# The odd layer's output projection in two halves of rows, one of them laid as half-token pieces into the ticks of differential attention

## The chip, the cores and the metric

The kernel runs on one NeuronCore of a Trainium2 chip. The metric is device time in microseconds (us). The engines are TensorE (PE, matmuls; PEld are its weight loads), VectorE (DVE), ScalarE (ACT), GpSimd (POOL) and SyncE (SP, which issues the weight DMAs). DVE, ACT, POOL and PE each run their own list of instructions in order, and semaphores tie the lists together.

## What is computed

One inference step of a two-layer decoder trunk for 512 prompt tokens and 64 sample tokens (T = 576 columns), model width 1024. Each layer is FFN, token mixing, FFN, and a gated per-layer input, every one with a residual add. The odd layer mixes by differential attention (4 heads of 128) beside stick-breaking attention (8 heads of 64), and ends in one output projection over both:

```python
cq, ck, cv, sq, sk, sv = jnp.split(hn @ W['od_w_in'][j], SPLIT_ODD, axis=-1)
oc = diff attention of (cq, ck, cv), each head normed and scaled     # 512 features
os_ = stick-breaking attention of (sq, sk, sv)                       # 512 features
mix = jnp.concatenate([oc, os_], axis=-1).astype(hn.dtype) @ W['od_w_out'][j]
h = h + mix
```

The projection is thus a sum of two products: 512 rows of the weight by the differential half and 512 rows by the stick-breaking half.

## The kernel before

**Layout.** Features lie on the 128 partitions and tokens along the free dimension. A product of two fp32 matrices is made of three fp32r matmuls (`mm3`, L574 to L576): high times high, high times the rest, the rest times high. Each operand X is split into a rounded part (`xr`, `wr`) and the rest (`xl`, `wl`). One matmul covers `HALF` = 288 columns, so an output tile of 128 features over K input blocks is K x 2 halves x 3 matmuls.

**Weights.** They come in blocks of at most 2048 columns in two slots. SP loads a block into `raw[s]` (L446), ACT copies it rounded into `wr[s]` (`round_block`, L1124), POOL subtracts to get `wl[s]` (`low_parts`, L559). ACT rounds a block only when PE has done with what the slot held. For the odd output projection (phase `("out", 1)`) a block is two output tiles of 8 input blocks each, and there are four blocks.

**Order in the odd layer.** 22 ticks of stick-breaking attention (`sb_tick`), with the input projections of differential attention cut in pieces between them, 24 matmuls a piece; then 25 ticks of differential attention (N = 20 maps, four heads of four prompt blocks and one group of sample rows, `MAPS`, and 5 ticks to drain); then the head norms; then the output projection. In tick t

- PE makes the scores of map t (L1039, L1044 for sample rows, L1050 else), turns the probabilities of map t-3 into PSUM bank 4 or 5, in turn (`turn_rows`, L876, L878), and multiplies those of map t-4 with the values (L1069 for sample rows, L1078 else);
- DVE adds the bias and takes the maxima of map t (L2038, L2042), then makes the probabilities of map t-1 (`probs`: L2057 and L2059 for sample rows, L2063 to L2068 else);
- ACT takes the exponentials of map t (L1503) and copies the turned rows of map t-3 to `rowsT` (`copy_rowsT`, L343). At the end of each head it copies its output to `oq` (L1520), and the outputs of stick-breaking attention are split into `xr` and `xl` in ticks 3 to 7 (L1490 on ACT, L2136 on DVE).

The buffers `rows` and `rowsT` lie in the weights' slot 1 (`wr[1]`, `wl[1]`), so slot 1 holds no weights during these ticks. After them PE sums squares for the head norms (L1094), ACT takes logarithm and exponential (L1527, L1530), DVE scales each head (L2192), and ACT and DVE split it into `xr` and `xl` (L1490, L2136), each head in turn. PE begins the projection with the four stick-breaking blocks of tile 0, which are ready, and waits for the four heads one by one:

```python
gemm(("out", 1), xin(5), lambda tile, k: ("mix_ready", KD + k + 1) if tile == 0 else None)
```

For each of the 8 output tiles DVE adds the tile to `h` (L1971), ACT makes the rounded next input and the square (L1155, L1145), DVE makes the rest (L1572) and sums the square (L1581):

```python
e.tensor_tensor(two(h[:, j, :]), unit(j % 2), two(h[:, j, :]), ALU.add).then_inc(S("tile_evacuated"), 1)
rest(m, j)
add_square(m, j, False)
```

PE may start tile j when tile j-2 has been added.

Of the kernel before, what the change touches and what calls it, by code (L numbers as in the profile page):

```python
# [85 lines left out]
def schedule():  # L86
    Phase.blocks = Phase.tiles = 0
    ph = {}
    order = []

    def add(name, *a):
        ph[name] = Phase(*a)
        order.append(name)

    def ffn(n):
        at = 0
        for c, k in enumerate(CHUNKS):
            add(("up", n, c), "up", n * sum(CHUNKS) + at, k, (KD, KD))
            at += k
            add(("down", n, c), f"down{c}", n * KD, KD, (k,))  # L100

    for l in range(2):
        ffn(2 * l)
        if l == 0:
            add("glu", "mixin", 0, 4, (KD, KD))
            add("kv", "mixin", 4, 4, (KD, KD))
            add("qo", "mixin", 8, 4, (KD, KD))
        else:
            add("qk1", "mixin", 18, 4, (KD, KD))
            add("v1", "mixin", 22, 2, (KD, KD))  # L110
            add("qk0", "mixin", 12, 4, (KD, KD))
            add("v0", "mixin", 16, 2, (KD, KD))
        add(("out", l), "mixout", l * 4, 4, (KD, KD))
        ffn(2 * l + 1)
        add(("ple", l), "ple", l * KD, KD, (KD, KP))
    return ph, order

def build(nc, A):
# [60 lines left out]
    def x_slot(m):  # L180
# [41 lines left out]
    z = [ZONE]  # L222
    oq = [sb(f"oq{i}", [P, TM, T], at=z) for i in range(2)]
    ok = [sb(f"ok{i}", [P, TM, T], at=z) for i in range(2)]
    ov = [sb(f"ov{i}", [P, ST, DA], at=z) for i in range(2)]
    qs = sb("qs", [P, HEADS, NB, 2, TB], at=z)
    nones = sb("nones", [P, P], at=z)
    identr = sb("identr", [P, P], F32R, at=z)
# [10 lines left out]
             for k in range(2)]  # L239
# [14 lines left out]
    qbd = sb("qbd", [P, 2, 5 * 64], at=z2)  # L254
    assert z2[0] <= XR_AT + 2 * KD * T * 4

    rows, rowsT = ([nc.alloc_sbuf_tensor_at(f"{n}{k}", [P, SEQ], F32, offset=W_AT[1] + (q * 4 + k) * SEQ * 4)
                    for k in range(4)] for q, n in enumerate(("rows", "rowsT")))
    assert 4 * SEQ <= BLK
    rows2 = [tg, sg, tu, hd]  # L260
    srow = sq
    assert max(ENDS) <= END, ("zone", [END - x for x in ENDS])
# [57 lines left out]
    def sample_softmaxes(u):  # L320

        return sum(m[3] == SAMPLES for m in MAPS[:min(u, N)])

    def score_bank(u, c):

        return 2 * (u % 2) + c
# [5 lines left out]
    def copy_rowsT(e, u):  # L332

        e.wait_ge(S("rows_turned"), u + 1)
        if u >= 4:
            e.wait_ge(S("values_done"), u - 3)
        dst, b = rowsT[u % 4], 4 + u % 2
        w = width(u)
        if MAPS[u][3] == SAMPLES:
            w = NPG * 64  # L340
            e.activation(dst[0:SMP, w:w + 64], ps[0:SMP, b, w:w + 64], ACT.Copy).then_inc(S("rowsT_part"), 1)
            e.wait_ge(S("rowsT_part"), SAMPLE_AT.index(u) + 1)
        e.activation(dst[:, 0:w], ps[:, b, 0:w], ACT.Copy).then_inc(S("probsT_copied"), 1)  # L343
# [97 lines left out]
    def _(e):  # L441
# [8 lines left out]
        def load_pair(p, i):  # L450
            for s in range(2):
                load_block(p, i, s)
# [48 lines left out]
        def load_odd(p, p0, pv):  # L501

            load_pair(p0, 0)
            e.wait_ge(S("pages_loaded"), 16)
            e.wait_ge(S("tile_done"), done_at("qk1", 0))
            load_sb_keys(0)
            load_sb_keys(1)
            load_pair(p0, 1)
            load_sb_keys(2)
            load_sb_keys(3)  # L510
            load_block(pv, 0, 0)
            load_sb_keys(4)
            load_sb_keys(5)
            load_sb_keys(6)
            load_block(pv, 0, 1)
            load_sb_keys(7)
            load_sb_values(0)
            load_block(p, 0, 0)
            load_sb_values(1)
            load_sb_values(2)  # L520
            load_block(p, 0, 1)
            for b in range(3, NB):
                load_sb_values(b)
            load_strips()
            for pair in range(PAIRS):
                if pair < 2:
                    e.wait_ge(S("sb_summed"), nth(NU))
                    e.wait_ge(S("sb_values_done"), units_before(NU, PROMPT))
                    e.wait_ge(S("sb_values_used"), NB)
                else:  # L530
                    e.wait_ge(S("values_done"), SAMPLE_AT[pair - 2] + 1)
                load_cache(pair)
            with e.Fori(1, p.nb // 2) as i:
                load_pair(p, i)

        for name in order:
            p = ph[name]
            if name in ("qk0", "v0"):
                continue
            if name == ("out", 1):  # L540
                load_odd(p, ph["qk0"], ph["v0"])
                continue
            with e.Fori(0, p.nb // 2) as i:
                load_pair(p, i)
# [25 lines left out]
    def _(e):  # L570
# [296 lines left out]
        def turn_rows(u, src, w, other=None):  # L867

            e.wait_ge(S("probs_done"), u + 1)
            if u >= 2:  # L870
                e.wait_ge(S("probsT_copied"), u - 1)
            nblk = (w + P - 1) // P
            for b in range(nblk):
                wb = min(P, w - b * P)
                if other is None:
                    mm = e.transpose(ps[0:wb, 4 + u % 2, b * P:(b + 1) * P], src[:, b * P:b * P + wb], C("ident"))  # L876
                else:
                    mm = e.matmul(ps[0:wb, 4 + u % 2, b * 64:(b + 1) * 64], src[:, b * P:b * P + wb], other,  # L878
                                  start=True, stop=True)
            mm.then_inc(S("rows_turned"), 1)  # L880

# [135 lines left out]
            sb_tick(k)  # L1017
        e.wait_ge(S("turned_copied"), 32)

        for tick in range(N + 5):  # L1020
            if tick < N:
                u = tick
# [11 lines left out]
                if i == SAMPLES:  # L1034
                    bank = score_bank(u, 0)
                    both = [(b, slice(64 * b, 64 * b + 64)) for b in range(2)]
                    for hh_ in range(HEADS):
                        for b, r in both:
                            e.matmul(ps[r, bank, 0:PAST], qbd[:, b, hh_ * 64:(hh_ + 1) * 64],  # L1039
                                     kc[hh % 2][:, b, hh_, :, :].rearrange("p g s -> p (g s)"),  # L1040
                                     start=hh_ == 0, stop=hh_ == HEADS - 1)
                    for hh_ in range(HEADS):
                        for b, r in both:
                            mm = e.matmul(ps[r, bank, PAST:KEYS], qbd[:, b, hh_ * 64:(hh_ + 1) * 64],  # L1044
                                          ok[0][:, hh_, SEQ:T], start=hh_ == 0, stop=hh_ == HEADS - 1)
                    mm.then_inc(S("scores"), 1)
                else:
                    for c_ in range(2):
                        r = slice(64 * c_, 64 * c_ + 64)
                        e.matmul(ps[:, score_bank(u, c_), 0:w], oq[0][r, hh, i * P:(i + 1) * P],  # L1050
                                 ok[0][r, hh, 0:w], start=True, stop=True).then_inc(S("scores"), 1)
            if 3 <= tick < N + 3:
                u = tick - 3
                turn_rows(u, rows[u % 4], width(u), C("fold") if MAPS[u][3] == SAMPLES else None)
# [41 lines left out]
            mm.then_inc(S("oc_ss"), 1)  # L1096
        e.wait_ge(S("oc_logged"), 2)

        gemm(("out", 1), xin(5), lambda tile, k: ("mix_ready", KD + k + 1) if tile == 0 else None)
        ffn(3, 6)  # L1100
        ple(1)
        norm_sum(8)
# [3 lines left out]
    def _(e):  # L1106
# [260 lines left out]

        def out_phase(name, m):

            for n in blocks(name):  # L1370
                for j in (2 * n, 2 * n + 1):
                    head(m, j, (S("tile_evacuated"), evac_at(name, j)))
                    square(m, j, None)

# [105 lines left out]
        def mixed_high(j):  # L1480
# [8 lines left out]
                src = oq[0][:, j - HEADS, :]  # L1489
            e.activation(xr[:, j, :], src, ACT.Copy).then_inc(S("mixr_ready"), 1)  # L1490

        for k in range(SB_TICKS):
            sb_act(k)
        for t in range(4):
# [2 lines left out]
        for tick in range(N + 5):  # L1497
# [23 lines left out]
                                 ).then_inc(S("attn_copied"), 1)  # L1521
            if 3 <= tick < 3 + HEADS:
                mixed_high(tick - 3)
        for hh in range(HEADS):
            buf = rows2[hh]
            e.wait_ge(S("oc_ss"), hh + 1)
# [5 lines left out]
                mixed_high(HEADS + hh - 1)  # L1532
        mixed_high(KD - 1)

        out_phase(("out", 1), 6)
        e.wait_ge(S("kv_stored"), 32)
        ffn(3, 6)
        ple(1)
# [12 lines left out]
    def _(e):  # L1551
# [587 lines left out]
        def copy_sb_samples():  # L2139
# [8 lines left out]
            settle()  # L2148
            ins.then_inc(S("sb_samples_copied"), 1)

        hg = tiny[:, 32:32 + HEADS]
        step(e.tensor_scalar(hg, W("head_g", 0, HEADS), 1.0 - LAM_INIT, None, ALU.mult))
        sb_queries()
# [3 lines left out]
            e.wait_ge(S(f"v_stored{t}"), 32)  # L2157
        e.wait_ge(S("turned"), 16)
        odd_tables()
        sample_queries(0)  # L2160
        for tick in range(N + 5):
            if tick < N:
# [19 lines left out]
                copy_sb_samples()  # L2182
            if 4 <= tick < 4 + HEADS:
                mixed_low(tick - 4)
        e.wait_ge(S("attn_copied"), HEADS)
        e.wait_ge(S("sample_copied"), PAIRS)
        e.wait_ge(S("rows_turned"), N)
# [6 lines left out]
            if hh:  # L2194
                mixed_low(HEADS + hh - 1)
        mixed_low(KD - 1)
        out_and_norm(("out", 1), 6)
        ffn(3, 6)
        ple(1)
        e.wait_ge(S("root_ready"), 9)  # L2200
# [164 lines left out]
```

## Time and profile before

| | us |
|---|---|
| median of 3 runs | 2659.73 (2658.12 to 2660.66) |
| the profiled execution | 2663.18 |
| its span in the trace | 2661.4 |
| ticks of differential attention in the trace | 2013.76 to 2097.57 |
| output projection, first matmul to last tile done | 2104.51 to 2156.5 |

Times in the trace count from the start of the span. In the trace's groups a line such as "2113.45 3.43 DVE L1572" is one instruction or a run of like ones: start, duration, engine, source line, operation, output from inputs.
### The profile page before, as it was taken

The numbers are of one execution on the slowest core, as the hardware profiler recorded it, in microseconds if no ns is written. First come the engines' busy times: TensorE is split into PE (matmuls) and PEld (weight loads), VectorE is DVE, ScalarE is ACT, GpSimd is POOL, SyncE is SP. The second block draws the span as 40 slices with busy tenths as digits, with TensorE's granted clock in tenths as the row PEclk, the third lists the DMA queues.
The fourth block names the chain that finished last, engine by engine and source line by source line (L and its number), as shares of the span: only waits on it lengthen the run. The fifth ranks groups of instructions, "written<-read, shape, count | busy, mean of one in ns | idle before, by whom it ended". The sixth has DMA issues, their size and how long they took to land.

```text
span 2661.4 us, 44264 instructions
## 1 busy us (share of the span) xinstructions
PE 2553.7 (96%) x18378; PEld 2436.5 (92%) x18378; DVE 816.2 (31%) x1383; ACT 762.6 (29%) x895; POOL 810.3 (30%) x210
## 2 busy tenths in 40 slices
PE   7999999998789999999999999999997999999997
PEld 7999999986489999999999999998774799999997
DVE  3220222686642211223322022212224522102233
ACT  4221224222523221224422122322232432212233
POOL 3333333321023333333333333431110133343332
PEclk9999999988889999999999999999998999999998
DMA  4223213411112222222221221232124122222222
GB/s 152 79 80 104 79 60 115 88 49 47 50 66 80 79 71 95 87 68 79 99 79 67 93 93 61 97 122 88 64 80 133 66 91 81 75 89 84 70 79 75
DMA packets 67829, 220.85 MB, mean 83 GB/s; under 512 B 13894, under 2 KB 33222, under 8 KB 52106
## 3 DMA queue, kind: packets, MB, share of 16 engines
q1 hardware_dynamic: 51104, 200.61, 21.9%
q10 hardware_dynamic: 16618, 18.70, 2.5%
q8 instruction: 82, 1.34, 0.2%
q14 instruction: 25, 0.20, 0.0%
HBM read 207.95 MB, written 11.33 MB: 82 GB/s over the span
## 4 chain that ended last, share of the span: by engine, by line
issue 79%; POOL 15%; PE 4%; DMA 0%; POOLq 0%; ACT 0%; DVE 0%; SPq 0%; DVEq 0%; ACTq 0%
POOL wl L559 15%; PE ps L574 1%; PE ps L575 1%; PE ps L576 1%; POOLq L565 0%; DMA raw<-in_up 0%; DMA kring<-in_kc 0%; ACT wr L1124 0%; DVE h L2206 0%; PE ps L888 0%; PE ps L634 0%; POOLq L555 0%; PE ps L931 0%; PE ps L891 0%; PE ps L946 0%
## 5 line engine op out<-in xcount | busy, mean ns | idle before, releaser
L559 POOL TENSOR_TENSOR wl<-raw,wr 128x2048 fp32r<-128x2048 f32 (+3 forms) x206 | 810.1, 3934 | 1824.0 <-ACT wr L1124 1824.0
L574 PE MATMUL ps<-xr,wr 128*128 128x288 f32 x4096 | 1219.7, 298 | 30.8 <-POOL wl L559 24.8
L575 PE MATMUL ps<-xl,wr 128*128 128x288 f32 x4096 | 1215.2, 297 | 0.0
L576 PE MATMUL ps<-xr,wl 128*128 128x288 f32 x4096 | 1212.8, 296 | 0.0
L574 PEld LDWEIGHTS ps<-xr,wr 128*128 128x128 f32 x4096 | 776.0, 189 | 36.8 <-issue 27.9
L575 PEld LDWEIGHTS ps<-xl,wr 128*128 128x128 f32 x4096 | 776.4, 190 | 0.8
L576 PEld LDWEIGHTS ps<-xr,wl 128*128 128x128 f32 x4096 | 777.0, 190 | 0.0
L1124 ACT ACTIVATE wr<-raw 128x2048 fp32r<-128x2048 f32 (+1 forms) x200 | 351.8, 1759 | 326.0 <-PE ps L576 283.7
L575 PE MATMUL ps<-hl,wr 128*128 128x288 f32 x1408 | 415.3, 295 | 0.0
L576 PE MATMUL ps<-hr,wl 128*128 128x288 f32 x1408 | 415.0, 295 | 0.0
L574 PE MATMUL ps<-hr,wr 128*128 128x288 f32 x1408 | 413.2, 293 | 0.0
L574 PEld LDWEIGHTS ps<-hr,wr 128*128 128x128 f32 x1408 | 264.7, 188 | 0.9 <-issue 0.9
L575 PEld LDWEIGHTS ps<-hl,wr 128*128 128x128 f32 x1408 | 264.7, 188 | 0.0
L576 PEld LDWEIGHTS ps<-hr,wl 128*128 128x128 f32 x1408 | 264.5, 188 | 0.0
L1179 ACT ACTIVATE hr<-hd 128x576 f32 (+1 forms) x88 | 60.3, 686 | 570.7 <-DVE hd L1616 570.7
L1600 DVE TENSOR_TENSOR tu<-ps,R 128x576 f32<-128x576 f32 x96 | 72.7, 757 | 491.2 <-PE ps L576 491.2
L1600 DVE TENSOR_TENSOR tg<-ps,R 128x576 f32<-128x576 f32 x111 | 84.0, 757 | 337.8 <-PE ps L576 309.8
L1629 DVE SCALAR_TENSOR_TENSOR h<-ps,h 128x576 f32 x64 | 48.5, 758 | 411.7 <-PE ps L576 411.7
L1176 ACT ACTIVATE sg<-tg 128x576 f32<-128x576 f32 x88 | 60.5, 687 | 253.7 <-DVE tg L1600 253.6
L1155 ACT ACTIVATE xr<-h,prm 128x576 fp32r<-128x576 f32 (+1 forms) x64 | 49.7, 776 | 248.6 <-DVE h L1629 167.2
L1620 DVE TENSOR_TENSOR hl<-hd,hr 128x576 f32 x88 | 66.8, 759 | 90.6 <-ACT hr L1179 90.6
L1738 DVE SCALAR_TENSOR_TENSOR ps<-up,prm,ps 128x512 f32<-128x512 f32 x116 | 87.6, 755 | 3.4 <-DVE us L1774 0.9
(338 smaller groups left out, 1431.8 us busy)
## 6 DMA issues: line engine op xcount, KB each, us to landing
raw<-in_up SPq DMA_DIRECT2D x88, 1024.0 KB, 4.7
raw<-in_down SPq DMA_DIRECT2D x32, 768.0 KB, 4.3
raw<-in_mixin SPq DMA_DIRECT2D x24, 1024.0 KB, 4.7
raw<-in_down SPq DMA_DIRECT2D x32, 640.0 KB, 3.8
raw<-in_ple SPq DMA_DIRECT2D x16, 640.0 KB, 3.8
raw<-in_mixout SPq DMA_DIRECT2D x8, 1024.0 KB, 5.0
kring<-in_kc SPq DMA_DIRECT2D x16, 256.0 KB, 4.1
vring<-in_vc SPq DMA_DIRECT2D x16, 256.0 KB, 3.0
```

What stands on the lines that cost most here:

```text
L559: ins = e.tensor_tensor(wl[s][:, c], raw[s][:, c], wr[s][:, c].bitcast(F32), ALU.subtract)
L574: e.matmul(out, wrt, xrt, start=first, stop=False)
L575: e.matmul(out, wrt, xlt, start=False, stop=False)
L576: return e.matmul(out, wlt, xrt, start=False, stop=last)
L1124: e.activation(wr[slot][:, 0:w], raw[slot][:, 0:w], ACT.Copy).then_inc(S("w_rounded"), 1)
L1155: e.activation(xj, hj, ACT.Copy, scale=prm[:, bass.ds(j + g0, 1)]).then_inc(S("xr_ready"), 1)
L1176: e.activation(sg[:], tg[:], ACT.Silu).then_inc(S("silu_ready"), 1)
L1179: e.activation(hr[:, bass.ds(i * 2 + s, 1), :].rearrange("p a t -> p (a t)"), hd[:], ACT.Copy).then_inc(S("hr_ready"), 1)
L1600: ins = e.tensor_tensor(two(out), unit(u), two(R[:]), ALU.mult)
L1620: e.tensor_tensor(q, hd[:], r.bitcast(F32), ALU.subtract).then_inc(S("hidden_ready"), 1)
L1629: e.scalar_tensor_tensor(hj, unit(s), 0.5, hj, ALU.mult, ALU.add).then_inc(S("tile_evacuated"), 1)
L1738: a = e.scalar_tensor_tensor(outp, inp, w, accp, ALU.mult, ALU.add)
```

## The change

Phase `("out", 1)` becomes two phases, each over four input blocks, with two weight blocks of four tiles each. `out_sb` is the stick-breaking half: it is cut in 16 pieces of one tile and half the tokens (12 matmuls of 288 columns), one in each of the ticks 8 to 23, between the scores and the turning. A piece writes bank 5; DVE adds it to `h` at the end of its tick (`add_half`), and the next piece waits for that. `out_diff` is the rest, made where the whole projection was, with ACT's and DVE's norm work per tile as before. The turned rows use bank 4 alone, so turning map u waits until the rows of map u-1 were copied. `rows` and `rowsT` move to buffers of stick-breaking attention (`ok[1]`, `ov[1]`), and slot 1 holds weights in the ticks. ACT rounds the second block of `out_sb` at the end of tick 2 and the first of `out_diff` at the end of tick 16; POOL subtracts after each.

```diff
-        add(("out", l), "mixout", l * 4, 4, (KD, KD))
+        if l == 0:
+            add(("out", 0), "mixout", 0, 4, (KD, KD))
+        else:
+            add("out_sb", "mixout", 4, 2, (TM,) * 4)
+            add("out_diff", "mixout", 6, 2, (TM,) * 4)
...
+    ROWS_AT = z[0] - TM * T * 4
...
+    ROWST_AT = z[0] - ST * DA * 4
...
+    OUT_TICK = 8
+    OUT_BANK = 5
+    def out_piece(tick):
+        n = tick - OUT_TICK
+        return divmod(n, 2) if 0 <= n < 2 * KD else None
...
-        dst, b = rowsT[u % 4], 4 + u % 2
+        dst, b = rowsT[u % 4], 4
...
-            with e.Fori(1, p.nb // 2) as i:
-                load_pair(p, i)
...
-            if u >= 2:
-                e.wait_ge(S("probsT_copied"), u - 1)
+            if u:
+                e.wait_ge(S("probsT_copied"), u)
...
+        def out_half(t, hf):
+            p = ph["out_sb"]
+            s, within = t // 4, t % 4
+            if (t, hf) == (0, 0):
+                e.wait_ge(S("mix_ready"), KD + HEADS)
+            if hf == 0:
+                if within == 0:
+                    e.wait_ge(S(f"w_split{s}"), p.n0 // 2 + 2)
+                e.wait_ge(S("tile_evacuated"), p.t0 + t + CR_EVAC)
+            else:
+                e.wait_ge(S("half_added"), t + 1)
+            x0, x1 = hf * HALF, (hf + 1) * HALF
+            for k in range(TM):
+                a, b = (within * TM + k) * P, (within * TM + k + 1) * P
+                mm = mm3(ps[:, OUT_BANK, 0:HALF], wr[s][:, a:b], wl[s][:, a:b],
+                         xr[:, k, x0:x1], xl[:, k, x0:x1], k == 0, k == TM - 1)
+            mm.then_inc(S("tile_done" if hf else "half_done"), 1)
...
+            if out_piece(tick):
+                out_half(*out_piece(tick))
             if 3 <= tick < N + 3:
                 u = tick - 3
                 turn_rows(u, rows[u % 4], width(u), C("fold") if MAPS[u][3] == SAMPLES else None)
...
-        gemm(("out", 1), xin(5), lambda tile, k: ("mix_ready", KD + k + 1) if tile == 0 else None)
+        gemm("out_diff", lambda tile, k: (xr[:, TM + k, :], xl[:, TM + k, :]),
+             lambda tile, k: ("mix_ready", KD + TM + k + 1) if tile == 0 else None)
...
+        out_blocks = blocks("out_sb")
...
+            if tick in (2, OUT_TICK + KD):
+                next(out_blocks)
...
-        out_phase(("out", 1), 6)
+        out_phase("out_diff", 6)
...
+        def add_half(t, hf):
+            part = h[:, t, hf * HALF:(hf + 1) * HALF]
+            if hf:
+                e.wait_ge(S("tile_done"), done_at("out_sb", t))
+            else:
+                e.wait_ge(S("half_done"), t + 1)
+            e.tensor_tensor(part, ps[:, OUT_BANK, 0:HALF], part, ALU.add
+                            ).then_inc(S("tile_evacuated" if hf else "half_added"), 1)
...
+        e.wait_ge(S("kv_stored"), 32)
         sample_queries(0)
...
+            if out_piece(tick):
+                add_half(*out_piece(tick))
...
-        out_and_norm(("out", 1), 6)
+        out_and_norm("out_diff", 6)
```

The weights in HBM are laid out to match, four tiles of four input blocks to a block; the bytes are the same.

## Rows read from the trace of the kernel before

**Rows 1.** The page's first line.
```profile
span 2661.4 us, 44264 instructions
```

**Rows 2.** Three stretches: length, busy us (instructions) by engine, granted clock, DMA share, GB/s.
```profile
core 0: us, PE busy (x) PEld busy (x) DVE busy (x) ACT busy (x) POOL busy (x), PEclk, DMA share, GB/s
2013.76:2046.91 33.15, 20.88 (x130) 11.91 (x129) 19.97 (x80) 10.82 (x36) 0.00 (x0) 0.69 0.40 129
2046.91:2097.57 50.66, 44.53 (x289) 25.76 (x288) 27.62 (x104) 23.03 (x73) 0.00 (x0) 0.93 0.31 104
2104.51:2156.50 51.99, 51.88 (x388) 51.57 (x387) 25.32 (x29) 21.56 (x26) 18.50 (x4) 1.00 0.22 80
```

**Rows 3.** Waits of PE, 2000 to 2110 us: total us, times, longest.
```profile
PE ps L1069 <- ACT oq L1520: 3.3, 2, 2.0
PE ps L1078 <- ACT rowsT L343: 2.9, 3, 2.4
PE ps L1078 <- DVE oq L2075: 2.2, 1, 2.2
```

**Rows 4.** Timeline of PE: three like groups, the values of sample rows.
```profile
2055.40 3.44 PE L1069 MATMUL ps<-vc,rowsT 128*32 128x512 f32 x8
...
2072.93 1.91 PE L1069 MATMUL ps<-vc,rowsT 128*32 128x512 f32 x8 [1.39 <-ACT oq L1520]
...
2088.92 3.35 PE L1069 MATMUL ps<-vc,rowsT 128*32 128x512 f32 x8 [1.96 <-ACT oq L1520]
```

**Rows 5.** Timeline of PE: first matmul of a 24-matmul piece, and its successor.
```profile
1934.17 0.35 PE L574 MATMUL ps<-xr,wr 128*128 128x288 f32 x1
...
1937.50 0.66 PE L971 MATMUL ps<-pweights,ov 128*64 128x128 f32 x8
```

**Rows 6.** Timeline around the output projection: PE's first matmul, then DVE.
```profile
2104.51 0.51 PE L574 MATMUL ps<-xr,wr 128*128 128x288 f32 x1
...
2108.96 1.60 DVE L2136 TENSOR_TENSOR xl<-oq,xr 128x576 fp32r<-128x576 f32 x2
...
2111.78 0.76 DVE L1971 TENSOR_TENSOR h<-ps,h 128x576 f32<-128x576 f32 x1 [0.62 <-PE ps L576]
...
2118.11 0.76 DVE L1971 TENSOR_TENSOR h<-ps,h 128x576 f32<-128x576 f32 x1 [0.56 <-PE ps L576]
...
2156.51 0.76 DVE L1971 TENSOR_TENSOR h<-ps,h 128x576 f32<-128x576 f32 x1 [2.80 <-PE ps L576]
```

**Rows 7.** Timeline of ACT, POOL and DVE in the projection's first tiles.
```profile
2109.67 1.90 ACT L1124 ACTIVATE wr<-raw 128x2048 fp32r<-128x2048 f32 x1
...
2111.65 4.62 POOL L559 TENSOR_TENSOR wl<-raw,wr 128x2048 fp32r<-128x2048 f32 x1 [129.28 <-ACT wr L1124]
...
2113.45 3.43 DVE L1572 SCALAR_TENSOR_TENSOR xl<-h,prm,xr 128x576 fp32r<-128x576 f32 x1 [0.91 <-ACT xr L1155]
...
2119.78 0.82 DVE L1572 SCALAR_TENSOR_TENSOR xl<-h,prm,xr 128x576 fp32r<-128x576 f32 x1 [0.91 <-ACT xr L1155]
2120.51 0.75 DVE L1581 TENSOR_TENSOR acc<-acc,sq 128x576 f32<-128x576 f32 x1
```

**Rows 8.** Timeline of ACT, DVE and PE in ticks 2 to 5.
```profile
2030.46 0.19 ACT L1503 ACTIVATION_READ_ACCUMULATOR rows<-rows,tiny 128x1 f32 x1
2032.40 0.61 ACT L1503 ACTIVATE rows<-rows,tiny 128x384 f32<-128x384 f32 x1 [1.76 <-DVE tiny L2038]
...
2032.95 0.45 DVE L2059 TENSOR_SCALAR rows<-rows,tiny,nlam 128x320 f32<-128x320 f32 x1
...
2033.61 0.25 ACT L343 ACTIVATE rowsT<-ps 128x128 f32<-128x128 f32 x1
...
2034.83 1.52 PE L878 MATMUL ps<-cst,rows 128*128 128x64 f32 x6
...
2035.75 0.36 ACT L343 ACTIVATE rowsT<-ps 128x256 f32<-128x256 f32 x1
```

**Rows 9.** DVE's groups by line and form, 2000 to 2111 us: busy us, mean ns.
```profile
L2065 DVE TENSOR_SCALAR rows<-rows,tiny 128x512 f32<-128x512 f32 x4 | 1.9, 486 | 0.1
...
L2068 DVE SCALAR_TENSOR_TENSOR rows<-sg,tiny,rows 128x512 f32<-128x512 f32 x1 | 0.8, 752 | 0.0
```

More of the change, by code:

```diff
@@ L255, in build @@
     assert z2[0] <= XR_AT + 2 * KD * T * 4
-    rows, rowsT = ([nc.alloc_sbuf_tensor_at(f"{n}{k}", [P, SEQ], F32, offset=W_AT[1] + (q * 4 + k) * SEQ * 4)
-                    for k in range(4)] for q, n in enumerate(("rows", "rowsT")))
-    assert 4 * SEQ <= BLK
+    rows, rowsT = ([nc.alloc_sbuf_tensor_at(f"{n}{k}", [P, SEQ], F32, offset=at + k * SEQ * 4)
+                    for k in range(4)] for n, at in (("rows", ROWS_AT), ("rowsT", ROWST_AT)))
+    assert 4 * SEQ <= TM * T and 4 * SEQ <= ST * DA
     rows2 = [tg, sg, tu, hd]
@@ L539, in _ @@
                 continue
-            if name == ("out", 1):
+            if name == "out_sb":
                 load_odd(p, ph["qk0"], ph["v0"])
@@ L875, in turn_rows @@
                 if other is None:
-                    mm = e.transpose(ps[0:wb, 4 + u % 2, b * P:(b + 1) * P], src[:, b * P:b * P + wb], C("ident"))
+                    mm = e.transpose(ps[0:wb, 4, b * P:(b + 1) * P], src[:, b * P:b * P + wb], C("ident"))
                 else:
-                    mm = e.matmul(ps[0:wb, 4 + u % 2, b * 64:(b + 1) * 64], src[:, b * P:b * P + wb], other,
+                    mm = e.matmul(ps[0:wb, 4, b * 64:(b + 1) * 64], src[:, b * P:b * P + wb], other,
                                   start=True, stop=True)
@@ L1368, in out_phase @@
         def out_phase(name, m):
+            per = ph[name].T
             for n in blocks(name):
-                for j in (2 * n, 2 * n + 1):
+                for j in range(per * n, per * (n + 1)):
                     head(m, j, (S("tile_evacuated"), evac_at(name, j)))
@@ L2302 @@
     a["mixin"] = np.concatenate([pairs(ev_t), pairs(np.concatenate([cq, ck, cvv, sq_, sk, sv]))])
-    a["mixout"] = np.concatenate([pairs(tiles_of(I["ev_w_out"][0], KD)), pairs(tiles_of(np.concatenate([I["od_w_out"][0][DA:], I["od_w_out"][0][:DA]]), KD))])
+    quads = lambda t: t.reshape(2, 4, P, 2, TM * P).transpose(3, 0, 2, 1, 4).reshape(4, P, BLK)
+    a["mixout"] = np.concatenate([pairs(tiles_of(I["ev_w_out"][0], KD)), quads(tiles_of(np.concatenate([I["od_w_out"][0][DA:], I["od_w_out"][0][:DA]]), KD))])
     wg = np.zeros((P, KD, 36), np.float32)
```

## The prediction

> **What bounds the kernel now.** I read the page first: its span is 2661.4 us [rows 1], and the profiled execution took 2663.18 us, 3.45 more than the median of the runs, 2659.73; the sum below is made on the former and shifted by 3.45 at the end. 0.2% is 5.3 us, about what a measurement of this kernel can tell from no change.
>
> Then I read the stretches around the change [rows 2]. The output projection, 2104.51 to 2156.50, is TensorE's: busy for 51.88 of 51.99 us at full clock. The reader should see that the ticks are close to it too. In ticks 8 to 23, where the pieces go (2046.91 to 2097.57, 50.66 us), PE is busy for 44.53 us, DVE for 27.62 and ACT for 23.03. So PE has only some 6 us to give away there, and the pieces bring 16 x 12 matmuls. Ticks 0 to 7 have more room (20.88 of 33.15) but get no piece. The granted clock is 0.93 in ticks 8 to 23, so a little time is lost at 1.2 GHz.
>
> The waits of PE [rows 3] say where the room is: 3.3 us in two waits for the copy of a head's output (ticks 15 and 20), 2.2 us for DVE's copy of the sample rows (tick 9), and 2.9 us for `rowsT`, of which 2.4 in one wait at tick 4, ahead of the pieces. That is 3.3 + 2.2 + 0.5 = 6.0 us in the pieces' ticks. The timeline puts a wait's start at a matmul's modelled end; the array could have taken the next instruction some 0.2 us earlier, so five waits give 1.0 more.
>
> **The change part by part.**
>
> *Pieces.* In the projection the 8 tiles of 48 matmuls follow each other every (2156.51 - 2118.11) / 6 = 6.4 us [rows 6], or 0.133 us a matmul; 12 are 1.6 us. What a piece costs among other work is shown where 24 matmuls stand in a stick-breaking tick: 1934.17 to 1937.50, 3.33 us [rows 5], 0.13 over 24 x 0.133. I take 1.6 + 0.14 = 1.74 us, 16 x 1.74 = +27.8 us. Bounds: 1.6, and 1.86, where a piece's two ends each cost 0.13.
>
> *Room they fill.* 6.0 + 1.0, less 0.3 at tick 9, whose DVE chain is longer than a piece: -6.7 us. The chains behind the other waits run under one or two pieces. `add_half` adds at most 0.76 us to a DVE tick (the 576-column L1971 is twice as wide [rows 6]), and DVE has 23 us free; it hides under the next turning and values.
>
> *Clock.* Two of three like groups of sample values took 3.44 and 3.35 us, the third 1.91 [rows 4]; the slow ones follow PE's long waits. The pieces fill these waits and may win 1.53 + 1.44 = 3.0 us. But other stretches with pieces also ran partly at half clock, so I take half: -1.5 (0 to -3.0).
>
> *Projection afterwards.* Tile 0 is done at about the same time as before. The last two heads are split at 2108.96 to 2110.56 [rows 6], and six matmuls (0.8 us) remain: 2111.4, against L1971's start at 2111.78. What ran under this chain before, tile 0's stick-breaking half, was free there and is paid for in the ticks. Tiles 1 to 7 take 3.2 us each in place of 6.4: -22.4, with tile 0 -22.6 us.
>
> *The norm work per tile.* DVE's part does not halve: L1971 to L1572 is 2119.78 - 2118.11 = 1.67 us, L1572 to L1581 0.73 and L1581 itself 0.75 [rows 6, 7], 3.1 us a tile. Before, that was half of a tile's 6.4 us; now it is all of the 3.2. And it can be held up: L1572 took 0.82 us alone and 3.43 us when POOL's L559 (2111.65, 4.62 us) was running, ending 0.61 us after it; L1971, which reads PSUM, took 0.76 us under the same L559 [rows 6, 7]. Two such subtractions fall into this phase. The first runs as before and puts DVE 2.6 us back: L1581(0) ends at 2117.6, tile 1 is added by 2118.3, and tile 3, which could start at 2117.9, stands for 0.4. The second follows tile 3: added by 2124.4, next input and square on ACT until 2125.9, ACT's rounding 1.90 [rows 7] until 2127.8, POOL until 2132.4. L1572 of tile 4 comes at 2128.5 and ends at 2133.1, L1581 at 2133.8, tile 5 is added by 2134.5. Tile 7, which could start at 2131.1, waits for that: 3.4 us. Together 3.8, of which 0.1 is regained by DVE: +3.7 us (0 if DVE gets ahead, 4.3 as the most). PE stood still for 2.0 to 2.2 us before the half-clock groups [rows 3, 4]; after 3.4 us I expect the clock to fall, +1.2 (0 to 1.7).
>
> *One PSUM bank.* The copy that turning u now waits for is the one that the next multiplication waits for anyway, so where a piece precedes it, it costs nothing. Ticks 4 to 7 have no piece: the turning at 2034.83 now waits for the copy that ends at 2036.11 [rows 8], +1.3 us (0 to 1.5).
>
> *Rounding in the ticks.* ACT's list ends tick 2 at 2030.65 and begins the next exponential at 2032.40 after 1.76 idle us [rows 8]; the rounding (1.90) covers that and costs 0.2 at the most. POOL then subtracts from 2032.6 to 2037.2. At 2032.95 stands L2059, which scales the probabilities of the sample rows. No row shows such an op, one SBUF tensor in, under L559. It costs nothing if it passes, and 2037.25 - 2032.95 = 4.3 us if it is held. Its kin L2065 takes 486 ns for 512 columns where L2068 with two tensors takes 752 [rows 9]: it moves faster than one element at a time would, and stands nearer to the ops that need more than one way into SBUF. I take "held". Behind it stand the maxima and exponentials of tick 4 and the copy of 2035.75 that both the turning and the values of tick 5 wait for, so PE's tick 5 starts up to 5.6 us late. I take +5.0 for tick 2 and the single bank together (1.3 to 5.6).
>
> The Trainium skill (SBUF — State Buffer, section "Who interferes with whom") says that VectorE and GpSimd share a pair of SBUF ports under an exclusive lock, taken by ops with two SBUF inputs against a GpSimd op that reads SBUF, and also by `tensor_scalar` in a two-port mode. This trace agrees on the former (3.43 against 0.82 us) [rows 7], and no row shows the latter. By the page the sum is the one forecast here; by the held rows alone it would be 3.7 us less.
>
> The subtraction after tick 16 starts while DVE waits for the scores of tick 18 behind two pieces, and ACT's rounding there runs under a piece: 0. The weights' DMAs are the same four, issued in the same order on SP; the store of `ok[1]` that DVE now waits for was issued long before: 0.
>
> *Sum.* 27.8 - 6.7 - 1.5 - 22.6 + 3.7 + 1.2 + 5.0 = +6.9 us. 2663.18 + 6.9 - 3.45 = **2666.6 us**, 0.26% slower.
>
> **Rivals.**
>
> *L2059 passes under POOL.* The 5.0 becomes 1.3: +3.2, 2662.9 us, no change that can be told. For it: every row that is held has two SBUF inputs. Against it: L2065's rate [rows 9]. Chance 0.25.
>
> *DVE is not late in `out_diff`.* It would need the second subtraction to miss L1572 of tile 4. Then 3.7 + 1.2 fall away: +2.0, 2661.7 us. Against it: the order on ACT is fixed, with the rounding between tile 3's square and tile 4's input. Chance 0.12.
>
> *Pieces sink into gaps between groups (the other side).* If a piece's ends replace a gap of 0.2 us that PE has at each end anyway, it costs 1.74 - 0.4 = 1.34: 21.4 in place of 27.8. With L2059 passing and the clock at 1.00 in the ticks: 21.4 - 6.7 - 3.0 - 22.6 + 3.7 + 1.2 + 1.3 = -4.7. It decides for "faster" from 1.30 us a piece on. For it: PE's busy time contains filling. Against it: the piece of 3.33 us, where nothing sank [rows 5]. At 1.25, 2653.8 us. Chance 0.08.
>
> *Clock falls more often.* With short pieces between small matmuls, nothing regained in the ticks, the second stall paid fully (1.7) and pieces at 1.86: 6.9 + 1.5 + 0.5 + 1.9 = +10.8, 2670.5 us. Chance 0.05.
>
> **How the numbers follow.** The forecast has 0.50. Its bounds (clock, bank, piece) give about 3 us to each side, so 0.35 of it is slower by over 5.3 us and 0.15 is not. Slower: 0.35 + 0.05 + 0.05 from the tails of the first two rivals = 0.45. Same: 0.15 + 0.30 = 0.45. Faster: 0.10, the third with a tail of the second. The range runs from between the third and second rival to beyond the fourth: 2656.5 to 2672.5; the forecast's own is 2663.5 to 2669.5.
>
> **What would show it.** Ticks 8 to 23 last some 70 us in place of 50.66, with PE's waits gone and clock near 1.00. L2059 in tick 3 lasts over 4 us. Turnings wait for L343 in ticks 4 and 5. In `out_diff`, two L1572 last 3 us or more, and PE waits for L1971 before tile 7. From the first matmul of `out_diff` to the next phase's, some 33 us. Wrong would make it: pieces much under 1.7 us, or L2059 at 0.45 us.

## The result, and the profile of the changed kernel

The changed kernel takes 2666.57 us (median of 16 runs, 2661.95 to 2674.01); the kernel before, run beside it as often, 2661.95 (2657.73 to 2666.20). The ratio is 1.0018, with a 95% interval of 1.0010 to 1.0027: 4.8 us slower, 2.7 to 7.2. The forecast was +6.9, and 2666.6 us.

The page's first line of the changed kernel [rows 1]; its execution took 2666.83 us.
```profile
span 2664.9 us, 44277 instructions
```

The same three stretches as in [rows 2]: ticks 0 to 7, ticks 8 to 23, and `out_diff`, with length, busy us (instructions), granted clock, DMA share and GB/s.
```profile
2013.76:2051.49 37.73, 20.47 (x133) 11.98 (x132) 23.80 (x80) 12.70 (x37) 4.51 (x1) 0.68 0.35 114
2051.49:2119.54 68.05, 66.74 (x481) 51.03 (x480) 34.63 (x120) 26.23 (x74) 4.57 (x1) 1.00 0.32 109
2126.76:2161.10 34.34, 30.71 (x213) 30.02 (x214) 25.16 (x28) 16.39 (x22) 9.23 (x2) 0.95 0.18 62
```
Ticks 8 to 23 grew from 50.66 us to 68.05, and TensorE is now busy there for 66.74 of them, at full clock (0.93 before). The stretch of the projection here ends with the last tile's sum on DVE; to the same point it took 52.76 us before (2104.51 to 2157.27), and takes 34.34 now. Tick 0 begins at 2014.16 in this trace, so ticks 0 to 7 last 37.33 us, 4.2 longer than before, although they hold no piece.

Line numbers moved: L559 is now L571, L1124 is L1158, L2059 is L2097, L876 and L878 are L888 and L890, L1069 and L1078 are L1102 and L1111, L343 is L357, L1572 is L1610, L1971 is L2009, L2136 is L2174; `add_half` is L2196 and the pieces are L586 to L588.

PE's waits, 2000 to 2165 us: total us, times, longest [rows 3].
```profile
PE ps L890 <- DVE rows L2106: 4.3, 1, 4.3
PE ps L586 <- DVE xl L2174: 3.3, 3, 1.6
PE ps L888 <- ACT rowsT L357: 2.9, 1, 2.9
PE ps L586 <- DVE h L2009: 2.0, 1, 2.0
...
PE ps L1111 <- ACT rowsT L357: 0.6, 1, 0.6
PE ps L586 <- DVE h L2196: 0.6, 2, 0.3
```
The waits for a head's copy (3.3) and for the sample rows (2.2) are gone; 1.2 us of waiting are left in the pieces' ticks. New are 4.3 us ahead of them and 2.0 us in the projection.

The timeline of ticks 2 to 5 says where the 4.3 come from [rows 8].
```profile
2031.02 1.90 ACT L1158 ACTIVATE wr<-raw 128x2048 fp32r<-128x2048 f32 x1
...
2032.99 4.51 POOL L571 TENSOR_TENSOR wl<-raw,wr 128x2048 fp32r<-128x2048 f32 x1 [50.26 <-ACT wr L1158]
...
2033.43 4.25 DVE L2097 TENSOR_SCALAR rows<-rows,tiny,nlam 128x320 f32<-128x320 f32 x1
2037.61 0.68 DVE L2076 CUSTOM_DVE_ANT_0 rows<-ps,strip 128x512 f32<-128x512 f32 x1
...
2039.75 0.36 ACT L357 ACTIVATE rowsT<-ps 128x256 f32<-128x256 f32 x1
...
2040.26 1.49 PE L890 MATMUL ps<-cst,rows 128*128 128x64 f32 x6 [4.34 <-DVE rows L2106]
...
2042.83 3.08 PE L1070 MATMUL ps<-kc,qbd 128*64 128x256 f32 x16
```
The scaling of the sample rows, 0.45 us before, takes 4.25 and ends 0.18 us after POOL's subtraction. Everything behind it on DVE is late, and the turning of tick 5, at 2034.83 before, comes at 2040.26. The bracket names L2106, which ended last; but that makes the rows of the next map. By the program this turning needs its own rows, scaled by 2037.68, and, with one bank, the copy of 2039.75 to 2040.11, which stands on ACT behind exponentials that wait for DVE. So hold and bank both stand in this wait.

A piece and the first of its successors, and the three groups of sample values [rows 4, 5]; the first group shows as a shorter run because two of its eight records are missing.
```profile
2052.50 0.40 PE L586 MATMUL ps<-xr,wr 128*128 128x288 f32 x1
...
2054.18 0.27 PE L888 MATMUL ps<-cst,rows 128*128 128x128 f32 x1
...
2063.60 1.46 PE L1102 MATMUL ps<-vc,rowsT 128*32 128x512 f32 x6
...
2085.62 1.91 PE L1102 MATMUL ps<-vc,rowsT 128*32 128x512 f32 x8
...
2107.69 1.91 PE L1102 MATMUL ps<-vc,rowsT 128*32 128x512 f32 x8
```
A piece costs 1.68 us from its first matmul to the next instruction's. The sample values that had taken 3.44 and 3.35 us run at full clock.

DVE and POOL in `out_diff` [rows 6, 7].
```profile
2133.86 0.76 DVE L2009 TENSOR_TENSOR h<-ps,h 128x576 f32<-128x576 f32 x1 [1.96 <-PE ps L588]
2135.53 2.09 DVE L1610 SCALAR_TENSOR_TENSOR xl<-h,prm,xr 128x576 fp32r<-128x576 f32 x1 [0.91 <-ACT xr L1189]
...
2147.39 0.75 DVE L2009 TENSOR_TENSOR h<-ps,h 128x576 f32<-128x576 f32 x1
2149.05 4.59 DVE L1610 SCALAR_TENSOR_TENSOR xl<-h,prm,xr 128x576 fp32r<-128x576 f32 x1 [0.91 <-ACT xr L1189]
2153.57 0.75 DVE L1619 TENSOR_TENSOR acc<-acc,sq 128x576 f32<-128x576 f32 x1
2154.23 0.75 DVE L2009 TENSOR_TENSOR h<-ps,h 128x576 f32<-128x576 f32 x1
```
DVE has no idle time beyond the 0.91 us per tile that it waits for ACT's rounded input. It adds a tile every 3.06 us, and every delay stays in it: 2.09 us in tile 0 and 4.59 in tile 4, each under a subtraction of POOL. After the second, PE waits 2.0 us for tile 5's sum before tile 7.

**The balance of the traces.** Single executions differ by some us before they come to the changed part (the shift against the kernel before at 1976 us lies between -3.9 and +10.5 us in the eleven traces beside it), so traces are compared piece by piece. The traces differ in clock, too: the two executions of one kernel in the table ("two pieces in the tail" and "the same again") differ by 1.0 us in A and by 1.0 in B, each time with 3.4 us more at half clock in the slower one, so a difference of less than about 1 us is not evidence by itself. A is the time from the first exponential of tick 2 to that of tick 8, B from there to the sum of tile 0 in the projection (L1971, L2009), C from there to DVE's first result of the next phase (`tg`). Before: 2029.99, 2048.57, 2111.78 and 2165.99 us, so A = 18.58, B = 63.21, C = 54.21. The table gives differences from these.

| kernel | A | B | C | A + B + C | ratio to before (95%) |
|---|---|---|---|---|---|
| changed | +4.12 | +17.50 | -20.06 | +1.56 | 1.0018 (1.0010 to 1.0027) |
| early rounding | +1.22 | +17.10 | -18.13 | +0.19 | 0.9998 (0.9985 to 1.0011) |
| two banks | +3.89 | +16.77 | -17.82 | +2.84 | 1.0009 (0.9997 to 1.0021) |
| split subtraction | +1.91 | +17.50 | -21.53 | -2.12 | 0.9994 (0.9983 to 1.0004) |
| before, one bank | +0.82 | -0.22 | 0.00 | +0.60 | one execution, 2669.72 us |
| before, rounding at tick 2 | +3.35 | +0.06 | -0.01 | +3.40 | one execution, 2666.32 us |
| the three edits together | -0.01 | +17.53 | -21.53 | -4.01 | 0.9989 (0.9977 to 1.0002) |
| and two pieces in the tail | -0.95 | +13.38 | -21.41 | -8.98 | 0.9977 (0.9962 to 0.9992) |
| the same again | +0.08 | +14.41 | -21.15 | -6.66 | 0.9971 (0.9953 to 0.9989) |
| and four pieces ahead of tick 2 | -0.39 | +7.97 | -21.39 | -13.81 | 0.9940 (0.9919 to 0.9961) |

### The profile page after: what moved, and what is told of

The parts are those of the page before. It is cut to its first block, busy times and chain, and to the rows that moved or that the text cites. A ratio compares the mean times of both kernels' runs of the same rounds, so it can differ in the third digit from the quotient of the medians.

```text
span 2664.9 us, 44277 instructions
## 1 busy us (share of the span) xinstructions
PE 2551.5 (96%) x18378; PEld 2437.8 (91%) x18378; DVE 827.5 (31%) x1399; ACT 764.2 (29%) x895; POOL 810.3 (30%) x210
## 4 chain that ended last, share of the span: by engine, by line
issue 72%; POOL 15%; PE 10%; DVE 1%; DMA 1%; ACT 1%; POOLq 0%; SPq 0%; DVEq 0%; ACTq 0%
POOL wl L571 15%; PE ps L586 2%; PE ps L587 2%; PE ps L588 2%; PE ps L900 1%; PE ps L1003 1%; PE ps L958 0%; PE ps L1070 0%; PE ps L1102 0%; POOLq L577 0%; DMA raw<-in_up 0%; ACT wr L1158 0%; PE ps L964 0%; PE ps L903 0%; PE ps L983 0%
## 5 line engine op out<-in xcount | busy, mean ns | idle before, releaser
L571 POOL TENSOR_TENSOR wl<-raw,wr 128x2048 fp32r<-128x2048 f32 (+3 forms) x206 | 810.1, 3934 | 1827.5 <-ACT wr L1158 1827.5
L586 PE MATMUL ps<-xr,wr 128*128 128x288 f32 x4096 | 1222.8, 299 | 37.0 <-POOL wl L571 25.0
L588 PE MATMUL ps<-xr,wl 128*128 128x288 f32 x4096 | 1213.9, 296 | 0.0
L586 PEld LDWEIGHTS ps<-xr,wr 128*128 128x128 f32 x4096 | 777.1, 190 | 49.9 <-issue 32.1
L588 PEld LDWEIGHTS ps<-xr,wl 128*128 128x128 f32 x4096 | 778.3, 190 | 0.0
L1158 ACT ACTIVATE wr<-raw 128x2048 fp32r<-128x2048 f32 (+1 forms) x200 | 351.9, 1760 | 326.0 <-PE ps L588 283.4
L588 PE MATMUL ps<-hr,wl 128*128 128x288 f32 x1408 | 415.0, 295 | 0.0
L586 PE MATMUL ps<-hr,wr 128*128 128x288 f32 x1408 | 413.2, 293 | 0.0
L586 PEld LDWEIGHTS ps<-hr,wr 128*128 128x128 f32 x1408 | 264.7, 188 | 0.9 <-issue 0.9
L588 PEld LDWEIGHTS ps<-hr,wl 128*128 128x128 f32 x1408 | 264.5, 188 | 0.0
```

Source lines behind the costliest of these rows:

```text
L571: ins = e.tensor_tensor(wl[s][:, c], raw[s][:, c], wr[s][:, c].bitcast(F32), ALU.subtract)
L586: e.matmul(out, wrt, xrt, start=first, stop=False)
L588: return e.matmul(out, wlt, xrt, start=False, stop=last)
L1158: e.activation(wr[slot][:, 0:w], raw[slot][:, 0:w], ACT.Copy).then_inc(S("w_rounded"), 1)
```

## Experiments

The theory is that of the prediction: TensorE pays every piece in the ticks, and POOL's subtractions, through DVE, add the loss at tick 3 and in `out_diff`. The rivals were the single bank as the cause of the early loss, pieces that sink into gaps, and a lateness of DVE that does not reach TensorE.

### Rounding before the ticks

```diff
         for k in range(SB_TICKS):
             sb_act(k)
+        next(out_blocks)
...
-            if tick in (2, OUT_TICK + KD):
+            if tick == OUT_TICK + KD:
```

> ACT's rounding of the second block of `out_sb`, and with it POOL's subtraction, is moved from the end of tick 2 to the end of the stick-breaking ticks, ahead of the first map of differential attention; nothing else is changed. Theory (POOL's subtraction of 4.5 us holds the scaling of the sample rows' probabilities, and the single PSUM bank costs only some 1 us): the scaling falls from 4.25 to about 0.45 us, the first matmul of tick 8, which is 3.9 us later than in the kernel before when both are set to tick 2, is only 0.5 to 1.5 us later, and the time is about 3 us below the changed kernel's. Rival (the single bank is what costs the 3.9 us): the scaling is short, but tick 8 stays 3 to 4 us late and the time does not change. Second rival (the lock moves elsewhere): some operation of DVE at the start of the ticks is now held for over 2 us and gives the 3 us back.

The turnings of ticks 4 and 5 in this run's timeline:
```profile
2034.22 0.41 PE L888 MATMUL ps<-cst,rows 128*128 128x128 f32 x2 [2.87 <-ACT rowsT L357]
2036.47 1.50 PE L890 MATMUL ps<-cst,rows 128*128 128x64 f32 x6 [1.20 <-ACT rowsT L357]
```
The scaling is back at 0.45 us and A falls from +4.12 to +1.22, as the theory has it: the hold is worth 2.9 us. What is left is the 1.20 us that the turning of tick 5 waits for the copy of tick 4, the price of the single bank. The time fell by 0.2% (1.0018 to 0.9998), somewhat more than 2.9 us but with intervals that touch. The trace's whole account fell by 1.4 us only, mostly because the clock fell in the projection after PE's wait, which it did not do in the changed kernel's trace (C).

### Two banks until tick 8

```diff
+    def turn_bank(u):
+        return 4 + u % 2 if u < OUT_TICK - 3 else 4
...
-            if u:
+            if u >= OUT_TICK - 3:
                 e.wait_ge(S("probsT_copied"), u)
+            elif u >= 2:
+                e.wait_ge(S("probsT_copied"), u - 1)
```

> The turning uses two PSUM banks in turn again for the maps turned before tick 8, and one bank from then on; the rounding at tick 2 stays. Theory (the hold under POOL is the larger part, and the turning of tick 5 then waits for the rows that this hold made late): the scaling stays at 4.25 us and tick 8 is 2.3 to 3.9 us late against the kernel before, so 0 to 1.6 us better than the changed kernel. Rival (the single bank is the cause): tick 8 is at most 1 us late, 3 us better than the changed kernel.

```profile
2034.55 1.52 PE L895 MATMUL ps<-cst,rows 128*128 128x64 f32 x6 [2.44 <-DVE rows L2102]
...
2038.12 3.68 PE L1075 MATMUL ps<-kc,qbd 128*64 128x256 f32 x16
```
Those are the turning of tick 5 and the first scores of tick 6 in this run's timeline. The turning waits for its own rows, whose scaling on DVE took 4.26 us; A is +3.89. The rival is out. That the second bank gave back only 0.2 us of A is the clock's doing: the scores of tick 6 begin 10.85 us after the exponential of tick 2, where the changed kernel needs 12.38, but from them to the values of the sample rows it is 5.25 us here, at half clock but for the last 0.1, and 3.95 there, 2.4 of them at half clock. So the bank is worth 1.5 us up to tick 6 with the hold, and as much without it: the scores of tick 6 come at 8.85 us with early rounding, and at 7.37 with two banks besides (the three edits together, below). The time, 1.0009, can't be told from the changed kernel's.

### POOL's subtraction in four instructions

```diff
+            if name in ("out_sb", "out_diff"):
+                low_parts(p, 0, 4)
+                continue
+            if name == ("up", 3, 0):
+                low_parts(p, 0, 4)
```

> Each of POOL's subtractions for the two halves of the projection (2048 columns in one instruction, 4.5 to 4.6 us) becomes four instructions of 512 columns, about 1.3 us each; the first pair of the phase that follows is split alike. Theory (DVE's operation waits for the whole of POOL's instruction that is running): the scaling in tick 3 and the held split of tile 4 take at most 1.8 us rather than 4.25 and 4.59, tick 8 is about 2 us less late, PE's wait of 2.0 us before tile 7 falls to 0 to 1, and the time falls by 2 to 4 us. Rival (DVE stays out for as long as POOL has anything to do): both stay over 4 us and the time is the same. Second rival (DVE's lateness does not reach PE in the projection): the operations are short, but the last tile is done at the same time.

POOL and DVE in this run's timeline, ticks 3 and 4, then the split of tile 4:
```profile
2032.12 5.16 POOL L571 TENSOR_TENSOR wl<-raw,wr 128x512 fp32r<-128x512 f32 x4 [49.30 <-ACT wr L1163]
...
2032.55 1.02 DVE L2102 TENSOR_SCALAR rows<-rows,tiny,nlam 128x320 f32<-128x320 f32 x1
...
2034.90 1.25 DVE L2108 TENSOR_SCALAR rows<-rows,tiny 128x384 f32<-128x384 f32 x1
...
2146.22 1.28 DVE L1615 SCALAR_TENSOR_TENSOR xl<-h,prm,xr 128x576 fp32r<-128x576 f32 x1 [0.91 <-ACT xr L1194]
```
Both of the theory's numbers came: 1.02 and 1.28 us where 4.25 and 4.59 stood, A at +1.91, no wait of PE for a tile's sum in the projection, and C at -21.53 in place of -20.06. So DVE gets in between two of POOL's instructions, and its lateness in `out_diff` was TensorE's. The time fell by 0.24%, to that of the kernel before: 6.4 us, more than the theory's 2 to 4, of which the trace's account shows 3.7.

### Pieces of three matmuls

```diff
-            for k in range(TM):
+            for k in range(1):
...
-                         xr[:, k, x0:x1], xl[:, k, x0:x1], k == 0, k == TM - 1)
+                         xr[:, k, x0:x1], xl[:, k, x0:x1], k == 0, k == 0)
```

> Each of the 16 pieces in the ticks has 3 matmuls in place of 12: three of the four input blocks of the stick-breaking half are left out of the result. Everything else is as in the changed kernel. Theory (TensorE is the bound of ticks 8 to 23, so that every matmul there is paid for at 0.133 us): ticks 8 to 23, 67.0 us with whole pieces and 49.5 in the kernel before, become 16 x 9 x 0.133 = 19.2 us shorter if all of it is paid, and less by what comes back of the waits (up to 6.7 us) and of the half clock (up to 3 us): 48 to 57 us. Rival (pieces sink into gaps, and what is paid is the joining of a tick to the next): the ticks become less than 8 us shorter, over 59 us.

PE's waits in ticks 8 to 23 of this run, and three stretches of its windows:
```profile
PE ps L586 <- DVE h L2196: 6.1, 6, 1.8
PE ps L1111 <- DVE oq L2113: 1.8, 1, 1.8
```
```profile
2070.88:2074.29 3.41, 3.41 (x11) 1.28 (x12) 2.25 (x9) 1.26 (x5) 0.00 (x0) 0.52 0.01 5
2091.36:2094.77 3.41, 3.41 (x11) 1.27 (x12) 1.88 (x7) 1.17 (x5) 0.00 (x0) 0.52 0.10 41
2111.84:2118.67 6.83, 6.43 (x17) 1.85 (x17) 2.15 (x6) 0.90 (x3) 0.00 (x0) 0.51 0.07 25
```
From the first scores of tick 8 (2062.11) to the last values (2123.24) it is 61.1 us, against 67.0 with whole pieces and 49.5 before: 5.9 us shorter, not 19.2. By the number the rival is right, by the trace it isn't: nothing sank into a gap. With short pieces, six of them wait for DVE to add the one before (6.1 us), one wait for the sample rows is back (1.8), and 13.65 us ran at half clock, which costs up to half of that. 19.2 saved, less 6.7 more of waits (7.9 against 1.2) and 6.8 for the clock, leaves 5.7. The waits came back as far as the theory allowed; the clock cost 6.8 us where it allowed 3. The full pieces hide a chain that lies close behind TensorE, and the theory that TensorE alone is the bound was too simple: it holds for pieces of 12 matmuls. This is one execution.

### One part alone in the kernel before

The single bank, with the waits of the change:
```diff
-        dst, b = rowsT[u % 4], 4 + u % 2
+        dst, b = rowsT[u % 4], 4
```

> The kernel before, with the turned rows in one PSUM bank as in the change, and nothing else of it. Theory (from the run with the early rounding, where tick 8 was 1.2 us later than before and nothing was held): tick 8, set to tick 2, is 1.0 to 1.5 us later than in the kernel before, one wait of the turning of tick 5 for the copy of tick 4 shows it, and in the ticks from 8 on, which have no pieces here, further waits of the turning appear, up to 3 us in all. Rival (the bank costs nothing without the pieces' other changes): tick 8 within 0.3 us.

A is +0.82, below the range; the turning of tick 5 waits 1.1 us. Behind tick 8 the turning waits 5.0 us for `rowsT`, in six waits, more than the 3 expected, but mostly in place of others: the sum of tile 0 is only 0.60 us late.

The rounding at tick 2, with the rows' buffers moved:
```diff
+            if tick == 2:
+                first_block = next(out_blocks)
...
-        out_phase(("out", 1), 6)
+        out_phase(("out", 1), 6, chain([first_block], out_blocks))
```

> The kernel before, with the buffers of the rows moved to those of stick-breaking attention, so that slot 1 can hold weights, and the second block of the projection rounded by ScalarE at the end of tick 2 rather than at the projection's start. No pieces, two banks for the turning. Theory (POOL's subtraction alone makes the early loss): the scaling of the sample rows takes about 4.2 us rather than 0.45, and tick 8, set to tick 2, is 3 to 4 us later than before; in the projection the first split, which took 3.43 us under POOL, takes 0.82. Rival (the loss needs the single bank as well): tick 8 at most 1.5 us later.

The scaling in tick 3, and the projection's first split, in this run's timeline:
```profile
2032.65 4.25 DVE L2064 TENSOR_SCALAR rows<-rows,tiny,nlam 128x320 f32<-128x320 f32 x1
...
2116.55 0.82 DVE L1577 SCALAR_TENSOR_TENSOR xl<-h,prm,xr 128x576 fp32r<-128x576 f32 x1 [0.91 <-ACT xr L1156]
```
With neither pieces nor a single bank, the moved subtraction alone makes A +3.35, and all of it is still there in the next phase (+3.40). In the projection, DVE saves 2.6 us that nobody waited for. Each alone, the bank and the rounding come to 0.82 + 3.35 = 4.17 us, and the changed kernel has 4.12: as far as single executions tell, the two losses add.

### The three edits together

> The changed kernel with three edits together: the second block of `out_sb` rounded before the ticks, two banks for the turning until tick 8, and POOL's subtractions of the two halves in four instructions each. Theory (the losses add up as the single runs showed them): tick 8, set to tick 2, is 0 to 0.5 us later than before (1.2 with the early rounding alone, of which the bank was the rest), ticks 8 to 23 are 17.5 us longer as in the changed kernel, the projection takes back 21.5, so that the next phase begins 3.5 to 4.5 us earlier than before, and the time is 3 to 5 us below that of the kernel before. Rival (early time that is won is lost again at the next wait): tick 8 stays 1 us or more late, or the ticks become longer by what was won, and the time is that of the run with the split subtraction alone.

Tick 8 is on the time of before (-0.01), B as in the changed kernel, C at -21.53: -4.01 us, inside the theory's range. The time is 0.11% (2.9 us) below that of the kernel before, at the edge of the 3 to 5 us expected, with an interval that just includes no change.

### Two pieces in the tail

```diff
+        out_half(KD - 1, 0)
         for hh in range(HEADS):
             e.wait_ge(S("oc_sq"), hh + 1)
+            if hh == 2:
+                e.wait_ge(S("half_added"), KD)
...
         e.wait_ge(S("oc_logged"), 2)
+        out_half(KD - 1, 1, 2)
```

> The three edits of the run above, and the last two pieces (both halves of tile 7) are taken out of ticks 22 and 23: one follows the last values, where TensorE waited 1.7 us for the squares of the heads, and one follows the sums of squares, in a free bank, where it waited 2.0 us for the first head. Theory (a piece costs 1.69 us in the ticks and nothing in a wait that it fits into): 2.5 to 3.4 us less than the run above before the projection's first matmul, and up to 1.3 us more if the fall of TensorE's clock after these waits is gone too: 2.5 to 4.7 us in all, the time 6 to 9 us below the kernel before. Rival (the waits there only seem free: VectorE's two more additions, 0.46 us each, stand in the heads' chain): 1 us or less.

> The run with the two pieces in the tail a second time, beside the one with the early pieces: 4 to 7 us below the kernel before, as the first time (0.9977).

PE's waits in this run, 2100 to 2160 us:
```profile
PE ps L594 <- DVE xl L2189: 1.7, 2, 0.9
...
PE ps L594 <- DVE h L2024: 0.2, 1, 0.2
```
The wait of 1.5 us for the squares and the longest one for a head are filled. B falls by 4.15 us against the run before (by 3.12 in the second run, where 2127.64 to 2131.05 ran at half clock, which the first did not). Both lie in the theory's 2.5 to 4.7. A's -0.95 in the first run is not the edit's: nothing before tick 8 was changed, and the second run has +0.08. The ratio is below 1 in both runs: 6.1 us, at the low end of the 6 to 9 expected, and 7.7 us (2.9 to 12.5), just above the 4 to 7 expected.

### Four pieces ahead of tick 2

```diff
+    EARLY = ((0, 0, 4), (0, 1, 6), (1, 0, 5), (1, 1, 7))
+    PIECE_TICKS = (9, 10, 11, 14, 15, 17, 18, 19, 20, 21)
...
+            if tick == 2:
+                for piece in EARLY:
+                    out_half(*piece)
+            if tick == 3:
+                e.wait_ge(S("tile_evacuated"), ph["out_sb"].t0 + 2 + CR_EVAC)
```

> The run above (three edits, two pieces in the tail), and four more pieces leave the ticks: tiles 0 and 1 are made ahead of the scores of tick 2, where TensorE waits 9.8 us for the keys in all the runs so far, in four banks that are free there, and added by VectorE at the end of tick 1. For that the stick-breaking outputs are copied and split before the ticks rather than in ticks 1 and 3 to 7, and the second block of `out_sb` is rounded at the end of tick 8. Ticks 8, 12, 13 and 16 then hold no piece, nor do 22 and 23. Theory (TensorE is the bound from tick 8 on and is idle before): tick 2 begins when its keys are there, as before, and the ticks from 8 on are 4 to 7 us shorter, so 3 to 8 us below the run above (2 us more if TensorE keeps its full clock into tick 2). Rival (VectorE becomes the bound of ticks 0 to 4: splits of 3 us and additions of 1.8 us stand ahead of its work there): tick 3's exponential is 2 to 5 us later than now against the arrival of the keys, and the gain is under 3 us.

PE's waits in this run, 2010 to 2125 us:
```profile
PE ps L595 <- DVE xl L2198: 4.9, 3, 3.2
PE ps L1131 <- ACT rowsT L361: 2.4, 1, 2.4
PE ps L1131 <- DVE oq L2137: 1.6, 1, 1.6
```
The wait of 9.8 us for the keys is gone; 3.2 us are left, for the first split. From the exponential of tick 8 to that of tick 19 the ticks are 5.4 us shorter than in the run above (44.81 against 50.24). The rival has a part: the pieces began at half clock (0.51 from 2018.81 to 2029.05), and tick 2, set to a rounding of ScalarE at 1976 us, is 1.5 to 1.7 us later than in the two runs above, against the theory, which had it begin as before. The table's A + B + C starts behind this delay; with it, the gain over the two runs above is 3.1 and 5.7 us, inside the theory's 3 to 8. The medians of the runs beside each other differ by 10.1 us (2659.25 and 2649.12), above that range; what the traces don't show of it stays open. The ratio of 0.9940 is the best of the study, about 16 us below the kernel before.

## Why the prediction was right, and where its sum was off

- *The time*: that 2666.57 us meets the forecast of 2666.6 so closely is luck. The kernel before, run beside it, took 2661.95 us and not the 2659.73 that the forecast stood on, and the change cost 4.8 us (2.7 to 7.2) and not 6.9; the two differences cancel. The direction holds.
- *Pieces*: 1.69 us each, 27.0 in place of 27.8. *Room*: TensorE's waits in these ticks fell from 6.1 us to 1.2, so 4.9 were seen to be filled; the forecast's 6.7 had 1.0 more for the modelled ends, which no run shows by itself. *Clock*: the whole 3.0 us came back, not half. 27.0 - 4.9 - 3.0 = 19.1; measured 17.5, from the first scores of tick 8 to the last values. The 1.6 between them are not assigned; with the forecast's 6.7 it would be 17.3.
- *One bank and rounding*: +4.1, inside the bounds (1.3 to 5.6), and its cause as chosen: L2059 is held under POOL. The Trainium skill (SBUF — State Buffer, section "Who interferes with whom") has `tensor_scalar` among the operations that can take the lock, and the lock lasting for the whole instruction. The trace now agrees on both: 4.25 us against 0.45, and 1.02 when POOL's instruction is a quarter as long.
- *Projection*: forecast -22.6 + 3.7 + 1.2 = -17.7, measured C = -20.06. The wait before tile 7 was 2.0 us, not 3.4, and that of 0.4 after tile 0 did not show. One fall of the clock was in no term: tile 0 ended on half clock, so its sum came 4.89 us behind the last head's scaling rather than 3.55. B has these 1.3 us, but does not show them, since the half clock that the norm work had before (0.50 from 2099.5 to 2102.9) was gone and gave 1.2 back. The later sum also let POOL hold the split of tile 0 for 2.09 us only, so that tile 1's sum came 4.35 us behind tile 0's rather than the forecast's 5.8. The clock did not fall after the wait before tile 7 in this execution; it did in those with early rounding and with two banks, where C is -18.13 and -17.82.
- *Sum*: the trace's own account is +1.56 us over the three pieces, against +6.9. The terms were off by -2.1 in the ticks, -0.9 at tick 3 and -2.4 in the projection. To the span's +3.5 come 0.46 us ahead of tick 2 and 1.5 in the gated input 430 us later, where the clock falls to 0.51 from 2598.17 to 2601.58. So the mechanism of one traced execution cost less than the medians show. The fall in the projection (1.5 us) would bring other executions nearer; no trace shows how often it happens, and this part stays open.
- *Rivals*: L2059 did not pass; DVE was late; nothing sank; the clock rose rather than fell in the ticks, but fell in tile 0. The third rival's time, at 1.25 us a piece, comes to 2653.6 us and not 2653.8.
- *Signs*: ticks 8 to 23 (68.05 us), L2059 and the wait before tile 7 came as named, and the turning of tick 4 waited 2.9 us for L343's copy; that of tick 5 waited for the copy too, as told above. Of the two splits only one lasted over 3 us (4.59; the other 2.09).

## What to carry to other kernels

Work moved into a stretch is free only in as far as the stretch has waits of the moved engine; 16 pieces of 1.69 us, 27.0 in all, got 9.5 us back from waits and lost clock, while a wait of 9.8 us six ticks earlier stayed empty. When a transfer or a rounding is moved, follow it to the last engine that it starts: here ScalarE's 1.90 us were hidden, and POOL's 4.5 us behind them held VectorE. Before you price a loss by a single run, ask what the clock did in it: the second bank was worth 1.5 us up to tick 6, and half clock left 0.2 of it.

## What the runs showed of the hardware that was not expected

- VectorE's operations with one input in PSUM ran at their usual time while POOL was subtracting without a break (0.68 us for 512 columns at 2033.49 with the split subtraction, as at 2037.61 in the changed kernel after POOL's end), and wide ones with all inputs in SBUF were held, not until POOL was through, but for about one of its instructions of 1.3 us: `tensor_scalar` of 320 and 384 columns took 1.02 and 1.25 us where 0.45 and 0.42 are usual. Those of one or two columns kept their time under POOL (the reciprocal 0.15 us at 2034.71, the scaling of one column 0.20 at 2036.08).
- A wait of some 1.9 us of TensorE is followed by half clock in some executions and not in others. At the start of the gated input it waits 1.9 us for POOL in the traces of the kernel before and of the changed one alike; the clock falls behind it in the latter alone, for 3.4 us. In the projection, 1.9 us were followed by a fall (early rounding) and 2.0 us were not (changed kernel).
